# Gated delta rule: the triangular inverse of levels 1 to 16 in compact 32x32 diagonal blocks, and a new order of the work around it

## What is computed

```python
def gated_delta_chunkwise(q, k, v, g, beta):
    ...
    kk = jnp.einsum("nbhld,nbhsd->nbhls", kc, kc)
    a_mat = jnp.where(strict, bc[..., :, None] * kk * decay, 0.0) + jnp.eye(L, dtype=jnp.float32)
    rhs = jnp.concatenate([vc * bc[..., None], kc * (bc * jnp.exp(G))[..., None]], -1)
    sol = lax.linalg.triangular_solve(a_mat, rhs, left_side=True, lower=True, unit_diagonal=True)
    ...
    def step(state, inp):
        u_, w_, attn_, qd_, kd_, gl_ = inp
        v_new = u_ - jnp.einsum("bhld,bhdv->bhlv", w_, state)
        o = jnp.einsum("bhld,bhdv->bhlv", qd_, state) + jnp.einsum("bhls,bhsv->bhlv", attn_, v_new)
        state = gl_[..., None, None] * state + jnp.einsum("bhld,bhlv->bhdv", kd_, v_new)
        return state, o
```

## Time and profile before

| | us |
|---|---|
| median of 3 runs | 1719.74 (1719.18 to 1723.5) |
| the profiled execution | 1719.42 |
| its span | 1717.6 |
| the delta stage in it | 131.7 to 325.4, that is 193.7 |

### The profile page before, as it was taken

The page is one execution under the profiler, slowest core; times in us unless marked ns, Lnnn a source line. Parts: engine busy times, 40 slices in busy tenths (PEclk is TensorE's granted clock), DMA queues, the critical chain, the costliest instruction groups (busy, mean ns, idle before and its releaser), DMA issues. The chain is left out here.

```text
span 1717.6 us, 23666 instructions
## 1 busy us (share of the span) xinstructions
PE 1667.9 (97%) x8218; PEld 1346.2 (78%) x8218; DVE 1064.1 (62%) x1716; ACT 849.4 (49%) x1453; POOL 440.6 (26%) x339
## 2 busy tenths in 40 slices
PE   9998999999999999989999999999999999999997
PEld 6786887878888888778888887888887876766775
DVE  6637455477666643588677748766664357888343
ACT  6756556354333432467556645433343245465673
POOL 1444445101111110035555620111111003232231
PEclk9999999999999999999999999999999999999999
DMA  5312112322333222311221212232322231221111
GB/s 219 123 61 75 37 38 68 107 96 74 98 98 98 87 96 98 110 62 50 74 74 50 74 60 101 74 98 98 98 85 98 98 110 65 99 74 62 62 62 49
DMA packets 40372, 144.25 MB, mean 84 GB/s; under 512 B 4562, under 2 KB 4818, under 8 KB 39780
## 3 DMA queue, kind: packets, MB, share of 16 engines
q1 hardware_dynamic: 40292, 143.20, 25.1%
HBM read 141.05 MB, written 2.13 MB: 83 GB/s over the span
## 5 line engine op out<-in xcount | busy, mean ns | idle before, releaser
L190 PE MATMUL bank<-u_high,w_high 128*128 128x512 f32 x1556 | 633.8, 407 | 5.9 <-PEq L1630 1.2
L192 PE MATMUL bank<-u_high,w_low 128*128 128x512 f32 x1556 | 607.9, 391 | 0.0
L191 PE MATMUL bank<-u_low,w_high 128*128 128x512 f32 x1556 | 607.0, 390 | 0.0
L190 PEld LDWEIGHTS bank<-u_high,w_high 128*128 128x128 f32 x1556 | 292.6, 188 | 81.1 <-issue 21.3
L192 PEld LDWEIGHTS bank<-u_high,w_low 128*128 128x128 f32 x1556 | 292.0, 188 | 63.2
L191 PEld LDWEIGHTS bank<-u_low,w_high 128*128 128x128 f32 x1556 | 292.9, 188 | 56.6 <-issue 3.1
L154 ACT ACTIVATE w_high<-w_ring 128x1024 fp32r<-128x1024 f32 x228 | 239.2, 1053 | 185.7 <-PE bank L192 160.8
L163 DVE TENSOR_TENSOR w_low<-w_ring,w_high 128x1024 fp32r<-128x1024 f32 x175 | 221.5, 1270 | 159.7 <-ACT w_high L154 159.2
L163 POOL TENSOR_TENSOR w_low<-w_ring,w_high 128x1024 fp32r<-128x1024 f32 x53 | 127.3, 2408 | 347.3 <-ACT w_high L154 347.3
L928 ACT ACTIVATE conv_up<-bank,col_sb 128x512 f32<-128x512 f32 x88 | 68.6, 779 | 263.5 <-DVE bank L988 263.5
L1057 POOL TENSOR_TENSOR hidden<-conv_up 128x512 f32 x44 | 58.2, 1323 | 488.0 <-DVE conv_up L999 364.1
(11 more groups left out here) (423 smaller groups left out, 2219.0 us busy)
## 6 DMA issues: line engine op xcount, KB each, us to landing
w_ring<-ffn_up SPq DMA_DIRECT2D x88, 512.0 KB, 3.5
w_ring<-ffn_down SPq DMA_DIRECT2D x44, 512.0 KB, 3.4
w_ring<-c_in SPq DMA_DIRECT2D x32, 512.0 KB, 3.5
w_ring<-g_in SPq DMA_DIRECT2D x16, 512.0 KB, 3.9
w_ring<-m_in SPq DMA_DIRECT2D x12, 512.0 KB, 8.1
w_ring<-fox_in SPq DMA_DIRECT2D x12, 512.0 KB, 3.6
w_ring<-dsa_in SPq DMA_DIRECT2D x12, 512.0 KB, 3.4
w_ring<-ab_out SPq DMA_DIRECT2D x8, 512.0 KB, 4.1
```

The lines of the kernel that those rows point to most:

```text
L190: nc.tensor.matmul(out, a[0], b[0], start=start, stop=False)
L191: nc.tensor.matmul(out, a[0], b[1], start=False, stop=False)
L192: return nc.tensor.matmul(out, a[1], b[0], start=False, stop=stop)
```

## The change

The levels 1 to 4 (block sizes 2 to 16) act only within the 32x32 blocks on the diagonal of each 128x128 chunk. The new kernel holds these blocks compactly: `Ac`, `Tc`, `Uc`, `Yc` are 128 x (4 chunks x 32). One level is then 16 matmuls of 32x32 with 32 columns, each at its own position (r, r) of the array, into one bank. Level 5 (32) and level 6 (64) compute only the corner that is not zero, with 8 and 12, and 4 and 4 small matmuls, from wide tiles `Un` and `Tn` into which the compact blocks are copied by six DVE copies after level 4. POOL's seven masked copies in halves become four compact ones per head (`masks`). The next head's `first_level` moves to just after `scores`. The fills are dealt out anew: the gate projection of the next head (8 units) stands in the levels, and all 24 units of slots 0 and 1 of head h + 2 and slot 2 of head h + 1 stand in the recurrence, 6 per chunk. ACT's `keys(n)` moves from the levels into the first chunk of the recurrence, `normalize` and `turn_o` of the head before into its second and third. A third gate tile and three more compact tiles are added, and 192 columns of constants.

```diff
@@ delta, tensor
-            def level(h, l, fill):
-                for a in range(2):
-                    pe.wait_ge(bt_ready, t_at(h, l, a))
-                    pe.wait_ge(t_ready, t_at(h, l - 1, a))
...
-                    for c in (2 * a, 2 * a + 1):
-                        ins = nc.tensor.matmul(b_y[a][:, cs(c)], bt(h, l)[:, cs(c)], tm(c), start=True, stop=True)
-                    ins.then_inc(y_done, 1)
...
+            def blockwise(bank, lhsT, rhs):
+
+                for c in range(NT):
+                    for r in range(P // B):
+                        ins = nc.tensor.matmul(bank[rows(r), c32(c)], lhsT[rows(r), c32(c)], rhs[rows(r), c32(c)],
+                                               start=True, stop=True, tile_position=(r * B, r * B))
+                return ins
+
             def level(h, l, fill):
+                pe.wait_ge(bt_ready, 4 * h + l)
+                pe.wait_ge(t_ready, t_at(h, l - 1))
+                blockwise(b4, BT[:, l - 1, :], Tc).then_inc(y_done, 1)
                 fill(l, 0)
+                pe.wait_ge(y_copied, y_at(h, l))
+                if l > 1:
+                    pe.wait_ge(u_ready, u_at(h, l - 1))
+                else:
+                    pe.wait_ge(*((s_ready, 3 * h) if h else (kdb_ready, 1)))
+                blockwise(b6, Uc, Yc).then_inc(z_done, 1)
...
+                gate_slots = [(1, 0), (2, 0), (3, 0), (4, 0)] if n == 1 else [(1, 0), (1, 1), (2, 0), (2, 1), (3, 0), (4, 0), (5, 0), (6, 0)]
+                chunk_units = [(s, g, m) for s, g in ((0, f), (1, f), (2, n)) for m in range(KD)]
...
                 def fill_chunk(c):
                     if f < H:
-                        project(*((1, f) if c < 2 else (2, n)), 4 * (c % 2), 4 * (c % 2) + 4)
+                        for s, g, m in chunk_units[6 * c:6 * c + 6]:
+                            project(s, g, m, m + 1)
@@ delta, scalar: recur
+                    if c == 0:
+                        keys(n)
+                    if c == 1:
+                        if f < H:
+                            high(2, n)
+                        if h:
+                            normalize(h - 1)
+                        if f < H:
+                            tap(f, 0)
@@ delta, vector
+                if l == 4:
+                    dve.wait_ge(u_ready, u_at(h, 4))
+                    dve.wait_ge(zeroed, 2)
+                    for r in range(P // B):
+                        nc.vector.tensor_copy(wide(Un)[rows(r), :, rows(r)], small(Uc[rows(r), :]))
+                    for r in range(HP // B):
+                        nc.vector.tensor_copy(Tn[rows(r), :, rows(r)], small(Tc[rows(r), :]))
```

More of the change, by code:

```diff
@@ L2092, in delta @@
     seq = {tile: n for n, tile in enumerate(order)}
[L2093 to L2096, removed]
+    t_at = lambda h, l: 5 * h + l + 1
+    u_at = lambda h, l: 4 * h + l
+    y_at = lambda h, l: 6 * h + l
+    pairs = [(slice(i, i + B), slice(i + B, i + 2 * B)) for i in (0, 2 * B)]
     col = lambda kind, h, c: k.cols[:, kind, h, c:c + 1]
@@ L2106, in mask, with c32, rows, small @@
         return k.c(name, lo, lo + P).rearrange("p (a l) -> p a l", a=1).to_broadcast([P, n, P])
[L2108 to L2116, removed]
+    def c32(c):
+        return slice(c * B, (c + 1) * B)
+    def rows(r):
+        return slice(r * B, (r + 1) * B)
+    def small(x):
+        return x.rearrange("p (c j) -> p c j", j=B)
+    def small_mask(name, l=0):
+        return k.c(name, l * B, l * B + B).rearrange("p (a j) -> p a j", a=1).to_broadcast([P, NT, B])
+    def wide(x):
+        return x[:, :].rearrange("p (c l) -> p c l", l=P)
     def b_out(h):
-        return b0 if h < H - 1 else b6
+        return b3 if h < H - 2 else b0 if h < H - 1 else b6
     def banks(h):
@@ L2644, in level @@
[L2644 to L2659 removed]
+                dve.wait_ge(masked, h + 1)
@@ L2680, in body @@
                 convolve(h, 2)
+                level(h, 2)
+                decays(n)
+                level(h, 3)
+                level(h, 4)
+                unit(n)
+                level(h, 5)
+                take_gate(n)
+                level(h, 6)
+                scores(n)
+                first_level(n)
+                state(h, 0)
+                if f < H:
+                    take(f, 0)
+                state(h, 1)
+                if f < H:
+                    convolve(f, 0)
+                    take(f, 1)
@@ L2681, in body @@
+                state(h, 2)
                 if h:
                     out(h - 1)
-                if n < H:
-                    decays(n)
-                level(h, 2)
-                mixing(1)
-                level(h, 3)
-                if n < H:
-                    unit(n)
-                mixing(2)
-                level(h, 4)
-                if n < H:
-                    take_gate(n)
-                    scores(n)
-                else:
-                    out_tiles.split_low(dve, 1, other=True)
@@ L2713, in body, with last_body @@
-                state(h, 2)
                 if f < H:
                     convolve(f, 1)
-                if n < H:
-                    first_level(n)
+                if h:
+                    dve.wait_ge(o_turned, h)
+                copy_out(h)
+            def last_body(h):
+                out_tiles.low(dve, 0)
+                take(h, 2)
+                level(h, 1)
+                convolve(h, 2)
+                out(h - 1)
+                level(h, 2)
+                out_tiles.low(dve, 1)
+                level(h, 3)
+                out_tiles.low(dve, 2)
+                level(h, 4)
+                out_tiles.split_low(dve, 1, other=True)
+                out_tiles.low(dve, 3)
+                level(h, 5)
+                out_tiles.split_low(dve, 2)
+                level(h, 6)
+                for j in (4, 5, 6):
+                    out_tiles.low(dve, j)
+                out_tiles.split_low(dve, 3)
+                for c in range(NT - 1):
+                    state(h, c)
+                copy_out(h)
@@ L2734, in _ @@
             convolve(1, 1)
-            for h in range(H):
+            for h in range(H - 1):
                 body(h)
+            last_body(H - 1)
             out(H - 1)
@@ L3324, in constants @@
     }
+    j = 32 * (s // 32) + np.arange(32)[None, :]
+    parts["small_levels"] = np.concatenate([parts["levels"][s, P * n + j] for n in range(5)], 1)
+    parts["small_ident"] = s == j
     return np.concatenate([np.asarray(parts[n], np.float32) for n, _ in _CST], 1)
```

317 lines of the change are left out of this document (156 added, 161 removed).

## The result

The changed kernel takes 1723.49 us (median of 20 runs, 1722.07 to 1731.44), the one before 1720.06 (its 20 runs 1719.18 to 1723.5). The ratio is 1.0028, 95% interval 1.0022 to 1.0035: 3.4 us slower, where 7 us faster was forecast. The profiled execution took 1723.59 with a span of 1721.7, at a mean granted clock of 0.987 (0.998 before). The stage's levels begin at the same time in both (y1 of head 0 at 152.83 and 152.79), and `turn_o` of the last head begins at 326.83 in place of 322.92, and from there to the end both take the same (1394.9 and 1394.7 us). So the loss of 3.9 us lies in the delta stage.

What follows compares the result with a forecast made beforehand. TensorE was taken as the bound, its clock staying at 1.00. Work 13.2 us less, waits 5.8 more and 0.3 for constants save 7.1: 1719.42 becomes 1712.3 profiled, 1712.6 median; range 1707 to 1731.

Steps and rivals of the forecast that it cites:

- The bound: Whole kernel: TensorE, busy 97% of the span; only shortening its instructions or waits can move the end.
- The price of a group: Levels 1 to 4: a compact group of small matmuls costs 0.67 us, against 0.89 before.
- The line drawn through the earlier trace: Small matmuls: start spacing of 0.82 ns per weight column, reaching 0.032 us at 32 columns.
- the fixed part from the earlier trace: Every new group: going into and out of a mode with array positions costs 0.35 us.
- 13.2 us less: Levels of all four heads: TensorE's cheaper groups save 3.3 us per head, 13.2 us in all.
- Rivals one and two: Level groups: positions run in sequence, 1.38 us each, 1733 (chance 0.18); or two at a time, 0.86, 1718.7 (0.15).
- The waits: Delta stage, four heads: TensorE's waits grow from 15.2 to 21.0 us, 5.8 more.
- Rival three: Levels 4 to 6: all six DVE copies meet POOL, y6 up to 1.8 us later in three heads; 1718, chance 0.12.
- four, with 0.05: Something else, such as the clock falling to 1.2 GHz in head 0's thinly filled levels; chance 0.05, no time given.
- The sum: Delta stage: 13.2 us less work, 5.8 more waits, 0.3 for constants if not free: 7.1 us saved.
- The range: Whole kernel: 1707 to 1731 us, leaving out most of the sequential-positions rival and the tails, no more than 0.2.
- The upper end of a group's price: Levels 1 to 4: 0.45 us of slots at 0.055 plus 0.35 fixed, 0.80 us per group.

Runs made afterwards that it cites:

- the run with the shorter chain: Changed kernel with ACT copying level 5 before exponentials and decay, and DVE updating level 5 before scaling k and q: 1716.49 us, ratio 0.9983.
- the padded one: Changed kernel with four plain fp32 128x128 matmuls, never read, behind each compact group of levels 1 to 4: 1735.27 us, ratio 1.0091.

## Why the prediction was wrong

**The bound.** Right: what moved the end was TensorE's work, its waits or its clock in every run. It was read too narrowly, though, as TensorE's work and its waits. Its speed was a third quantity.

**The price of a group.** The direction was right and the size not: 0.49 us in place of 0.67. The slots were right. The line drawn through the earlier trace rows gave 0.032 us; the 32 halves of a group start within some 0.27 us, which is eight slots of 0.033. What was too large was the fixed part from the earlier trace rows, 0.35, where 0.22 is left. The term "13.2 us less" should then have been larger by 0.18 x 32 = 5.8. Only some of that could reach the end: a group that gets shorter ahead of a wait makes the wait longer. The groups of level 6 were cheaper too: y6 in the run with the shorter chain costs 213.63 - 0.23 - 212.72 = 0.68, against 0.83.

**Rivals one and two** (positions one after the other, or in pairs; 0.18 and 0.15) are out. A window cut in the middle of y1 of head 1 shows 24 halves of the group started by 202.08, within 0.21 us of the first:

```profile
201.87 0.39 PE L2218 MATMUL bank<-g_T,g_BT 32*32 32x32 f32 x24
```

If the Trainium skill's floor of about 25 ns from start to start (TensorE: Matmul & The Clock Gate, "Wait — 56ns, not 53.3ns?") held for halves at different positions, they would by estimate have needed 0.6. The Trainium skill's rule that different row tiles cannot access one PSUM bank at once (TensorEngine Tiling (Array Packing), "Gotcha 1: PSUM Pressure") is not borne out for tiles on the diagonal either: these four write one bank. For such tiles the measurement decides against both.

**The waits.** This was the long part of the working, and in the main it held:

| wait of TensorE | forecast, us | measured, us |
|---|---|---|
| ahead of y6, heads 0 / 1 / 2 | 2.5 | 2.53 / 2.55 / 2.54 |
| first unit of head 2's recurrence | 2.7 | 2.74 |
| all of head 0 / 1 / 2 / 3 (that ahead of y1 of head 0, 0.83, included) | 6.9 / 3.4 / 6.1 / 4.6 | 7.7 / 3.8 / 6.6 / 5.1 |
| recurrence of heads 0 and 1 | 0 | none over 0.1 |

The sums are 21.0 and 23.2. Their parts fit less well than the sums. In head 0 the forecast had 2.7 us for Y of level 2 and nothing ahead of y2; measured were 1.25 ahead of y2 (for DVE) and 0.52 for Y of level 2. Ahead of z5 heads 1 and 2 wait 0.71 in place of 0.4, and ahead of y5 nothing in place of 0.2. Rival three (six copies against POOL, 0.12) is out too: four of the six met POOL, and the wait came out as forecast.

**The clock.** This is the step that failed. The sum has no term for a change of the clock; it went on at 1.00. It stood as a remainder, "four, with 0.05: ... a fall of the clock to 1.2 GHz in the thinly filled levels of head 0; before it stayed at 1.00 through every wait". The row was right and the inference from it wrong. Before, the waits stood between plain groups of 0.89 us and units. The change made the groups of levels 1 to 4 cost 0.49; it moved the units behind z1 and z2 of head 0 into levels 3 and 4, and took eight units out of levels 5 and 6 of heads 0 and 1; and it opened a wait of 2.5 us ahead of y6 in heads 0 to 2. That the kernel before keeps its clock through some 15 us of waits says nothing about one with less work between longer waits. The runs showed in its place 37.5 us of the stage at 0.50 and a price of 11.4 us by the medians. Nor was the place right: only 10.2 of the 37.5 us lie in the levels 1 to 4 of head 0, and 23.9 begin just ahead of y6 of heads 0 to 2. The Trainium skill states in general that the throttled state is the default and that activity releases it (TensorE: Matmul & The Clock Gate, "What's actually happening"); the trace agrees, at 0.50 in five stretches.

**The sum.** 1712.3 was forecast for the profiled execution and 1712.6 for the median. With the clock held up by matmuls that compute nothing, and all else as in the change, the median is 1712.12 and the heads take 43.5, 43.1 and 35.2 us, where 44, 44 and 36 were forecast. So apart from the clock the sum is within half a microsecond, but some of that is luck. In the profiles, y1 of head 0 to `turn_o` of the last head takes 170.1 us before, 174.0 in the changed kernel and 161.3 with the extra matmuls, where the sum makes it 163.0. The stage is 1.7 us better than the sum (the groups are cheaper, the waits a little longer, and a low stretch of 3.4 us is still left in head 3), y1 of head 0 comes 0.8 us earlier, and 2.0 us are lost again behind the stage, see below. The clock's price, 11.4 us by the medians and 12.7 in these profiles of the stage, outweighed the 7.1 that were to be gained. The range did hold the time, but only because rivals had widened it that did not come true.

**Slips in the working.** None of them decided anything. The upper end of a group's price takes a slot of 0.055 us "as at 66 columns", where the earlier trace rows give 0.060. The lower end of the forecast's own range is 1712.6 - 40 x 0.06 = 1710.2, not 1709. A group of 1.15 us in 32 places adds 15.4 us to the forecast, which makes the kernel 8.3 us slower than before, or about 6 with the 2 us that vanish behind ACT's roots, not 5.

**What stays open.** In six of the nine variants, the profiled execution has one more stretch of low clock, somewhere between 750 and 790 us, in a stage whose code is the same in all kernels; the profiles of before and of the changed kernel have none there. It has a price: from `turn_o` of the last head to the end take 1396.9 or 1397.0 us in the five variants where it lasts 6.8 us, 1395.2 where it lasts 3.4 (the padded one), and 1394.6 to 1394.9 in all the others. So these five gained some 2 us more in the delta stage than in the whole. Whether a shift in time brings it on was not tried. Nor was it tried whether it is the narrow matmuls or the idle time between them that lets the clock fall, or why it falls more in some executions of a kernel than in others.

## What to carry to other kernels

Ask of every change that takes work from TensorE, or moves it out of a stretch with waits, what TensorE still does there, and give the fall of its clock a mechanism, a place and a price of its own: the work in and right behind the stretch, once more (here keys of 1.9 us became 3.6). A wait can cost more than its own length, by the clock of the work behind it, and then work that needs doing anyway belongs in it; if there is none, a few matmuls that compute nothing are a cheap test and even a cure: 27 of them in three waits gave 8.5 us back. When such a fill makes a kernel faster, with the granted clock back at 1.00 and the other engines' busy time unchanged, the clock was the cost. Look at several executions, though: one trace shows one pattern of low stretches, and the same kernel has others.

## What the chip showed that was not expected

- fp32 matmuls of 32x32 at the four diagonal positions run beside each other into one bank: sixteen of them, 32 halves, cost 0.49 us ahead of a unit, where four matmuls of 128x128 cost 0.89.
- The low clock lasts well beyond the wait ahead of it: in head 0 it came right behind one of 1.25 us and stayed for 10.24 us, in which products, norms and small groups kept TensorE busy for 9.22. Two waits of 0.5 us lie within.
- Small copies of DVE on 32 partitions more than double beside a POOL operation, 0.92 to 2.11 us for four, as the larger ones in the earlier trace rows do.
